# Where the Griffin product and two weight low parts stand in VectorE's program, in a two-layer hybrid decoder trunk

## The chip, the cores and the metric

The kernel runs on one NeuronCore of a Trainium2 chip. The metric is the device time of one execution in microseconds (us). TensorE (PE in the profile) does the matrix products, VectorE (DVE) and ScalarE (ACT) the elementwise work, GpSimd (POOL) a smaller share of it, and SyncE (SP) issues the DMA transfers of the weights.

## The reference, cut to what matters

Two layers, each of them a half-weighted SwiGLU, a token mixer and another half-weighted SwiGLU, on 256 tokens of width 1024. The mixer runs four branches on one normed input: gated DeltaNet, a diagonal state space model (S5), Griffin's gated linear recurrence (RG-LRU) and retention. What the change touches is in two of them:

```python
def hybrid_mixer(hn, ...):
    proj = hn @ w_in          # all inputs of the branches, and the gates' logits
    out_a = gated_deltanet(...); out_b = s5_layer(...)
    out_c = rg_lru_block(...);   out_d = retention(...)
    gates = sigmoid(gate_logits)
    merged = sum(gates * (branches @ w_branch))
    return merged @ w_out

# gated DeltaNet, chunks of 64 tokens
rhs = concatenate([v * beta, k * (beta * exp(gc))])
lower = where(strict, beta * (k @ k.T) * decay, 0)     # decay = exp(gc_i - gc_j)
attn = (q @ k.T) * decay
q_dec = q * exp(gc)
k_dec = k * exp(gc[-1] - gc)
# Griffin
return h * gelu(yb)
```

## The kernel before, in words

Activations lie transposed in on-chip memory, channels on the partitions and the 256 tokens along a row. All weights are streamed from memory once per layer in pieces of 128 x 1024 values (512 KB). A product keeps nearly full float32 accuracy by three passes: weights and inputs are each split into a high and a low part, and `product` (L492 to L494) issues high by high, low input by high weight, high input by low weight.

**The stream of weights.** SP loads piece i into one of 3 slots of `raw`, once the low part of piece i-3 has been taken. ScalarE copies it to the high part `whi` (L908), once TensorE has used piece i-4. VectorE subtracts (`wlo = raw - whi`, L1265); GpSimd does that for a few pieces (L1174). TensorE waits for the low part before it uses a piece. Nothing schedules this by itself: each engine runs a list written out by hand, in which `ahead(unit)` and `split_to(n)` say up to which piece the high or low parts are made at that place. `ahead(unit)` means up to two pieces beyond the last one of that unit.

**The units.** Each `gate(i)` on TensorE is a projection of 256 gate channels: two pieces, g{i}.0 and g{i}.1, 24 products' passes each. Between the gates TensorE does the small products of the branches, the side units. They use three PSUM banks in turn, in a fixed order: ... eb, ktr, vtr, gb0, gb1, kk0, bb0, kk1, bb1, qk0, qk1 ... So gb1 has the bank of ktr, kk0 that of vtr, and bb1 that of kk0: TensorE waits at each until the engine that reads the earlier unit has done so.

**The place of the change.** After the input projections, of which rv is the last, TensorE does eb, gate 0, the transposes of keys and values (ktr and vtr, L663), the decay rows spread over the partitions (gb0 and gb1, in `over_all`, L671), gate 1, kk0, bb0, kk1, bb1 (keys against keys at L684, betas at L671), gate 2, qk0 and qk1 (L684), gate 3, and then six levels of a triangular inverse.

VectorE meanwhile finishes the normed queries and keys (L1536, L1537), forms Griffin's output (L1541, L1542), makes the low parts of g1.0 and g1.1, scales the queries (L1545, `qdec`), reads ktr's bank twice over for the scaled keys (L1558 and L1559, tile `qkvp`), reads vtr's bank for the scaled values (L1564), makes the low parts of g2.0 and g2.1, and reads gb0 and gb1 (L1580). Then it waits for the exponentials of ScalarE (L1107) and multiplies them with kk and bb (L1585 to L1590).

ScalarE evacuates each gate's bank (L1096) and splits Griffin's output for the later merge (L1103). That split is needed only in the merge, which follows gate 15.

Of the kernel before, what the change touches and what calls it, by code (L numbers as in the profile page):

```python
# [31 lines left out]
ALU = mybir.AluOpType  # L32
ACT = mybir.ActivationFunctionType
# [174 lines left out]
def trunk(nc, weights, params, consts, positions, x_in, y_out):  # L208
    ctx = ExitStack()
    with ctx:  # L210
# [6 lines left out]
        def sb(name, cols, dt=F32, over=None, skip=0):  # L217

            if over is None:
                place[name] = place[""]  # L220
                place[""] += -(-cols // 8) * 8
                assert place[""] <= SLAB, place[""]
            else:
                place[name] = place[over] + skip
            return nc.alloc_sbuf_tensor_at(name, [P, cols], dt, offset=base + 4 * place[name])

        def two(name, n=2, t=SEQ, dt=F32, over=None, skip=0):
            return sb(name, n * t, dt, over, skip)[:].rearrange("p (k t) -> p k t", k=n)
# [11 lines left out]
        griffin = wide[:, 30:32, :]  # L240
# [4 lines left out]
        qkv = two("qkv", 6)  # L245
        zz, su, ly = two("zz"), two("su"), two("ly")
# [5 lines left out]
        brh = sb("brh", 8 * SEQ, F32R, over="flat8")[:].rearrange("p (n k t) -> p n k t", n=NB, k=2)  # L252
# [21 lines left out]
        egb, qdec = two("egb"), two("qdec")  # L274
        rows, rowT = two("rows", 1)[:, 0, :], two("rowT", 2, P)
        tmpA, tmpB, tmpC, tmpD, tmpE, tmpF = (two("tmp" + c) for c in "ABCDEF")
# [14 lines left out]
        side = Units(SIDE, psum[4:7])  # L291
# [9 lines left out]
        def S(name):  # L301

            if name in once:
                return once[name]
            if (Now.layer, name) not in per_layer:
                per_layer[Now.layer, name] = nc.alloc_semaphore(f"{name}_{Now.layer}")
            return per_layer[Now.layer, name]

        def since(name, n):

            return once[name], Now.layer * PER_LAYER[name] + n
# [16 lines left out]
        def halves(ap, n=2):  # L328
            return ap.rearrange("p (k t) -> p k t", k=n)
# [39 lines left out]
        def slot(ring, i):  # L369
            s0 = (i % (RAW_SLOTS if ring is raw else SLOTS)) * SLOT  # L370
            return ring[:, s0:s0 + P * numbered(i)[1]]

        def piece_at(name):
            return Now.layer * NP + PIECE_INDEX[name]

        def last_piece(unit):
            return Now.layer * NP + UNIT_PIECES[unit][-1]
# [15 lines left out]
        def r32(ap):  # L393

            return ap.bitcast(F32)
# [495 lines left out]
        def scalar_layer(act):  # L891
            A = nc.scalar.activation
# [18 lines left out]
            def ahead(unit):  # L911

                split_to(last_piece(unit) + 3)
# [175 lines left out]
            def gate(i):  # L1089
                ahead(f"g{i}")  # L1090
                act.wait_ge(S("main"), main.ready(f"g{i}"))
                if i == 11:
                    act.wait_ge(*since("s5x", 8))
                if i == 15:
                    act.wait_ge(S("branch2"), 1)
                A(gates[:, 2 * i:2 * i + 2, :], halves(main.bank(f"g{i}")[:]), ACT.Tanh, scale=0.5).then_inc(S("main_act"), 1)  # L1096
# [2 lines left out]
            act.wait_ge(S("side"), side.ready("eb"))  # L1099
            A(egb, halves(side.bank("eb")[:]), ACT.Exp).then_inc(S("side_act"), 1)  # L1100
            gate(0)
            act.wait_ge(S("griffin"), 1)
            A(brh[:, 2], griffin, ACT.Copy).then_inc(S("branch_high"), 1)  # L1103
            ahead("g1")
            for hp in range(2):
                act.wait_ge(S("side_dve"), side.taken(f"gb{hp}"))
                A(flat(dec)[:, hp, :], flat(dec)[:, hp, :], ACT.Exp).then_inc(S("dec"), 1)  # L1107
            gate(1)
            gate(2)
            gate(3)  # L1110
            for lv in range(LEVELS):
# [138 lines left out]
        def vector_layer(dve):  # L1250
            V = nc.vector
            chain = [0]

            def link(ins):
                chain[0] += 1
                ins.then_inc(S("dve"), 1)
                dve.wait_ge(S("dve"), chain[0])
# [3 lines left out]
            def split_to(n):  # L1261

                for i in [i for i in range(split[0], min(n, DEPTH * NP)) if i % NP in BY_DVE]:
                    dve.wait_ge(once["high"], i + 1)
                    V.tensor_tensor(slot(wlo, i), slot(raw, i), r32(slot(whi, i)), ALU.subtract).then_inc(S("low_dve"), 1)  # L1265
                split[0] = max(split[0], n)

            def ahead(unit):

                split_to(last_piece(unit) + 3)  # L1270
# [265 lines left out]
            V.scalar_tensor_tensor(qkv[:, 0:2, :], qkv[:, 0:2, :], 0.5 * DH ** -0.5, mx_sq[:, 0:2, :], ALU.mult, ALU.mult)  # L1536
            V.scalar_tensor_tensor(qkv[:, 2:4, :], qkv[:, 2:4, :], 0.5, mx_sq[:, 2:4, :], ALU.mult, ALU.mult).then_inc(S("k_normed"), 1)  # L1537
            dve.wait_ge(S("k_normed"), 1)

            dve.wait_ge(S("gelu_t"), 1)  # L1540
            link(V.scalar_tensor_tensor(tmpD, tmpD, 1.0, ly, ALU.add, ALU.mult))  # L1541
            V.scalar_tensor_tensor(griffin, tmpF, 0.5, tmpD, ALU.mult, ALU.mult).then_inc(S("griffin"), 1)  # L1542
            ahead("g0")
            dve.wait_ge(S("side_act"), side.taken("eb"))
            V.tensor_tensor(qdec, qkv[:, 0:2, :], egb, ALU.mult).then_inc(S("dve_q"), 1)  # L1545

            dve.wait_ge(S("side"), side.ready("ktr"))
            dve.wait_ge(S("side_act"), side.taken("rowt"))
# [18 lines left out]
                link(V.tensor_copy(brh[:, n], src))  # L1567
                V.tensor_tensor(brl[n], src, r32(brh[:, n]), ALU.subtract).then_inc(S(f"branch{n}"), 1)

            ahead("g1")  # L1570
            dve.wait_ge(once["masks"], 4)

            for hp in range(2):
                ps = side.bank(f"gb{hp}")
                dve.wait_ge(S("side"), side.ready(f"gb{hp}"))
                for t in range(2):
                    for j in range(2):
                        o = (t * 2 + j) * 64
                        h = 2 * t + hp
                        last = V.tensor_scalar(dec[:, hp, t, j, :], ps[:, o:o + 64], rowT[:, j, h:h + 1], 0.0, ALU.subtract, ALU.min)  # L1580
                last.then_inc(S("side_dve"), 1)
            tj = lambda m, hp: m[:, hp].rearrange("p t j c -> p (t j) c")
            for hp in range(2):
                dve.wait_ge(S("dec"), hp + 1)
# [201 lines left out]
        with nc.Block() as block:  # L1786
# [14 lines left out]
            @block.vector  # L1801
            def _(dve):
                vector_first(dve)
                for Now.layer in range(DEPTH):
                    vector_layer(dve)
                vector_last(dve)

            @block.scalar
            def _(act):
                scalar_first(act)  # L1810
                for Now.layer in range(DEPTH):
                    scalar_layer(act)
# [167 lines left out]
```

## Time and profile before

| | before |
|---|---|
| median of 3 runs | 1367.34 us (1365.52 to 1367.47) |
| the profiled execution | 1367.37 us, span 1365.6 us |
| PE busy | 1318.3 us, 97% |
| DVE busy | 894.7 us, 66% |
| ACT busy | 646.7 us, 47% |
| POOL busy | 246.0 us, 18% |
| mean granted TensorE clock | 0.989 |

The span is the time from the first to the last instruction; 1.8 us of the execution lie outside it. The clock of 1.00 is 2.4 GHz, and 0.50 is 1.2 GHz. In the timeline rows, the first number is the start in us from the span's beginning, the second how long the row's instructions take together, and a bracket names idle time of the engine before it and what ended that.

### The profile page before, as it was taken

The page shows a single profiled execution, that of the slowest core. Times are in us where ns is not written, and L with a number is a line of the kernel's source. Part 1 is how long each engine was busy: PE and PEld are TensorE (multiplying, and loading weights), DVE is VectorE, ACT ScalarE, POOL GpSimd, SP SyncE. Part 2 cuts the span into 40 slices and gives each one's busy share as a digit, 9 for nine tenths or more (in the row PEclk, how much of TensorE's full clock was granted, in tenths as well). Part 3 has the DMA queues.
Part 4 walks back from the last instruction along what each step waited for, and adds up shares of the span by engine and source line. Part 5 has one row for each costly group of instructions (what it writes and reads, how often), then busy time and mean ns, then how long its engine had stood idle before and what let it go on. Part 6 is the DMA issues. An engine that isn't in the chain of part 4 may idle for free. (4 is left out here: it accounts for less than half of the span.)

```text
span 1365.6 us, 27564 instructions
## 1 busy us (share of the span) xinstructions
PE 1318.3 (97%) x11790; PEld 1280.6 (94%) x11790; DVE 894.7 (66%) x1343; ACT 646.7 (47%) x948; POOL 246.0 (18%) x199
## 2 busy tenths in 40 slices
PE   6999999989999999999999999999889999999998
PEld 6999999988788999999999999999877899999997
DVE  7777546876966865555477765568678577655553
ACT  6444647643234454444454455476322354544442
POOL 2000011004833520000210000200166254100000
PEclk9999999999999999999999999999999999999999
DMA  6555654533233545566546556454422335555553
GB/s 233 193 186 187 197 190 143 183 124 106 79 109 109 170 152 188 186 208 207 180 149 188 186 184 194 151 193 145 136 90 67 124 122 168 167 190 188 181 182 117
DMA packets 61321, 220.25 MB, mean 161 GB/s; under 512 B 6928, under 2 KB 7184, under 8 KB 60688
## 3 DMA queue, kind: packets, MB, share of 16 engines
q1 hardware_dynamic: 61200, 218.50, 49.7%
q8 instruction: 93, 1.52, 0.4%
q14 instruction: 28, 0.23, 0.1%
HBM read 217.42 MB, written 1.05 MB: 160 GB/s over the span
## 5 line engine op out<-in xcount | busy, mean ns | idle before, releaser
L492 PE MATMUL bank<-xh,whi 128*128 128x256 f32 x2384 | 676.6, 284 | 5.5 <-DVE wlo L1265 3.8
L493 PE MATMUL bank<-xl,whi 128*128 128x256 f32 x2384 | 669.6, 281 | 0.0
L494 PE MATMUL bank<-xh,wlo 128*128 128x256 f32 x2384 | 668.8, 281 | 0.0
L1265 DVE TENSOR_TENSOR wlo<-raw,whi 128x1024 fp32r<-128x1024 f32 (+1 forms) x382 | 469.2, 1258 | 159.7 <-ACT whi L908 157.6
L908 ACT ACTIVATE whi<-raw 128x1024 fp32r<-128x1024 f32 (+1 forms) x414 | 416.3, 1035 | 108.9 <-DMA raw<-weights 93.6
L492 PEld LDWEIGHTS bank<-xh,whi 128*128 128x128 f32 x2384 | 452.0, 190 | 14.0 <-issue 6.3
L493 PEld LDWEIGHTS bank<-xl,whi 128*128 128x128 f32 x2384 | 451.9, 190 | 0.2
L494 PEld LDWEIGHTS bank<-xh,wlo 128*128 128x128 f32 x2384 | 451.7, 189 | 0.0
L493 PE MATMUL bank<-hl,whi 128*128 128x256 f32 x704 | 196.8, 279 | 0.0
L494 PE MATMUL bank<-hh,wlo 128*128 128x256 f32 x704 | 196.6, 279 | 0.0
L492 PE MATMUL bank<-hh,whi 128*128 128x256 f32 x704 | 196.6, 279 | 0.0
L1215 POOL TENSOR_TENSOR flat<-flat 128x256 f32<-128x256 f32 x36 | 33.6, 932 | 714.7 <-ACT flat L927 713.7
L971 ACT ACTIVATE tmpB<-bank 128x256 f32<-128x256 f32 x88 | 33.8, 385 | 237.7 <-PE bank L494 237.5
L492 PEld LDWEIGHTS bank<-hh,whi 128*128 128x128 f32 x704 | 132.3, 188 | 0.0
L494 PEld LDWEIGHTS bank<-hh,wlo 128*128 128x128 f32 x704 | 132.3, 188 | 0.0
L493 PEld LDWEIGHTS bank<-hl,whi 128*128 128x128 f32 x704 | 132.3, 188 | 0.0
L1304 DVE TENSOR_TENSOR tmpC<-tmpB,bank 128x256 f32<-128x256 f32 x88 | 37.1, 422 | 132.5 <-ACT tmpB L971 132.5
L1174 POOL TENSOR_TENSOR wlo<-raw,whi 128x1024 fp32r<-128x1024 f32 x32 | 78.1, 2447 | 100.8 <-ACT whi L908 100.7
L927 ACT ACTIVATE flat<-x 128x512 f32<-128x512 f32 (+1 forms) x30 | 16.4, 546 | 101.4 <-DVE x L1322 101.4
L1096 ACT ACTIVATE wide<-bank 128x512 f32<-128x512 f32 x32 | 19.1, 597 | 82.6 <-PE bank L494 82.6
L1322 DVE SCALAR_TENSOR_TENSOR x<-bank,x 128x512 f32<-128x512 f32 (+1 forms) x30 | 17.5, 583 | 53.8 <-PE bank L494 53.8
L1193 POOL TENSOR_TENSOR big<-big,cst 128x256 f32<-128x256 f32 x24 | 16.8, 721 | 190.4 <-DVE big L1594 190.4
(351 smaller groups left out, 1261.1 us busy)
## 6 DMA issues: line engine op xcount, KB each, us to landing
raw<-weights SPq DMA_DIRECT2D x350, 512.0 KB, 4.0
raw<-weights SPq DMA_DIRECT2D x64, 448.0 KB, 3.9
cst<-consts SPq DMA_DIRECT2D x1, 1088.0 KB, 11.0
par<-params SPq DMA_DIRECT2D x1, 1072.5 KB, 7.5
par<-params SPq DMA_DIRECT2D x1, 1060.5 KB, 9.0
x<-x_in SPq DMA_DIRECT2D x1, 1024.0 KB, 5.1
y_out<-ret SPq DMA_DIRECT2D x4, 256.0 KB, 2.3
ropec<-positions SPq DMA_DIRECT2D x1, 128.0 KB, 2.1
```

What stands on the lines that cost most here:

```text
L492: mm(out, w[0], a[0], start=start, stop=False)
L493: mm(out, w[0], a[1], start=False, stop=False)
L494: return mm(out, w[1], a[0], start=False, stop=stop)
L908: A(slot(whi, i), slot(raw, i), ACT.Copy).then_inc(once["high"], 1)
L971: A(tmpB[:, m % 2, :], main.bank(f"gu{f}_{m}")[:, 0:SEQ], ACT.Silu).then_inc(S(f"silu{f}"), 1)
L1096: A(gates[:, 2 * i:2 * i + 2, :], halves(main.bank(f"g{i}")[:]), ACT.Tanh, scale=0.5).then_inc(S("main_act"), 1)
L1174: tt(slot(wlo, i), slot(raw, i), r32(slot(whi, i)), ALU.subtract).then_inc(S("low_pool"), 1)
L1193: tt(lowc[:, hp].rearrange("p t j c -> p (t j) c"), low[:, hp].rearrange("p t j c -> p (t j) c"), over(lev[:, lv, 0:64], 4), ALU.mult).the ...
L1215: tt(squared[:, 0, :], squared[:, 0, :], squared[:, k, :], ALU.add).then_inc(S("sq_step" if k < KD - 2 else "sq_added"), 1)
L1265: V.tensor_tensor(slot(wlo, i), slot(raw, i), r32(slot(whi, i)), ALU.subtract).then_inc(S("low_dve"), 1)
L1304: V.tensor_tensor(tmpC[:, m % 2, :], tmpB[:, m % 2, :], ps[:, SEQ:512], ALU.mult).then_inc(S("main_dve"), 1)
L1322: V.scalar_tensor_tensor(x[:, tiles, :], halves(main.bank(unit)[:, 0:n * SEQ], n), scale, x[:, tiles, :], ALU.mult, ALU.add).then_inc(S("m ...
```

## The change

VectorE's program, between the normed keys and the use of the decays: Griffin's product (L1541, L1542) and the scaled queries (L1545) move behind the eight reads of gb0 and gb1. The low parts of g1.0 and g1.1, which stood together ahead of the scaled queries, are taken apart: g1.0's stands ahead of ktr's scaling, g1.1's behind vtr's. Those of g2.0 and g2.1 move behind the scaled queries. ScalarE's split of Griffin's output moves from behind gate 0 to behind gate 1. Every instruction is still there once, with the same operands.

```diff
@@ ScalarE @@
             gate(0)
-            act.wait_ge(S("griffin"), 1)
-            A(brh[:, 2], griffin, ACT.Copy).then_inc(S("branch_high"), 1)
             ahead("g1")
             for hp in range(2):
                 act.wait_ge(S("side_dve"), side.taken(f"gb{hp}"))
                 A(flat(dec)[:, hp, :], flat(dec)[:, hp, :], ACT.Exp).then_inc(S("dec"), 1)
             gate(1)
+            act.wait_ge(S("griffin"), 1)
+            A(brh[:, 2], griffin, ACT.Copy).then_inc(S("branch_high"), 1)
             gate(2)
@@ VectorE @@
             dve.wait_ge(S("k_normed"), 1)
-
-            dve.wait_ge(S("gelu_t"), 1)
-            link(V.scalar_tensor_tensor(tmpD, tmpD, 1.0, ly, ALU.add, ALU.mult))
-            V.scalar_tensor_tensor(griffin, tmpF, 0.5, tmpD, ALU.mult, ALU.mult).then_inc(S("griffin"), 1)
-            ahead("g0")
-            dve.wait_ge(S("side_act"), side.taken("eb"))
-            V.tensor_tensor(qdec, qkv[:, 0:2, :], egb, ALU.mult).then_inc(S("dve_q"), 1)
+            split_to(piece_at("g1.0") + 1)
 
             dve.wait_ge(S("side"), side.ready("ktr"))
...
-            ahead("g1")
+            split_to(piece_at("g1.1") + 1)
             dve.wait_ge(once["masks"], 4)
...
                 last.then_inc(S("side_dve"), 1)
+            dve.wait_ge(S("gelu_t"), 1)
+            link(V.scalar_tensor_tensor(tmpD, tmpD, 1.0, ly, ALU.add, ALU.mult))
+            V.scalar_tensor_tensor(griffin, tmpF, 0.5, tmpD, ALU.mult, ALU.mult).then_inc(S("griffin"), 1)
+            dve.wait_ge(S("side_act"), side.taken("eb"))
+            V.tensor_tensor(qdec, qkv[:, 0:2, :], egb, ALU.mult).then_inc(S("dve_q"), 1)
+            ahead("g1")
             tj = lambda m, hp: m[:, hp].rearrange("p t j c -> p (t j) c")
```

VectorE's program before, from the instruction behind the normed keys to the first use of the decays (`wide` is Griffin's output, `wlo` a low part, `qkvp` the scaled keys and values, `big` the decays):

```order
L1541 SCALAR_TENSOR_TENSOR tmpD<-tmpD,ly 128x512
L1542 SCALAR_TENSOR_TENSOR wide<-tmpF,tmpD 128x512
L1265 TENSOR_TENSOR wlo<-raw,whi 128x1024 x2
L1545 TENSOR_TENSOR qdec<-qkv,egb 128x512
L1558 TENSOR_TENSOR qkvp<-bank,rowT 128x256
L1559 TENSOR_TENSOR qkvp<-bank,rowT 128x256
L1558 TENSOR_TENSOR qkvp<-bank,rowT 128x256
L1559 TENSOR_TENSOR qkvp<-bank,rowT 128x256
L1564 SCALAR_TENSOR_TENSOR qkvp<-bank,rowT 128x256 x2
L1265 TENSOR_TENSOR wlo<-raw,whi 128x1024 x2
L1580 TENSOR_SCALAR big<-bank,rowT 128x64 x8
L1585 TENSOR_TENSOR big<-big,cst 128x256
```

The same stretch of VectorE's program in the changed kernel (its line numbers are lower by 6 where the Griffin lines used to stand ahead):

```order
L1265 TENSOR_TENSOR wlo<-raw,whi 128x1024
L1552 TENSOR_TENSOR qkvp<-bank,rowT 128x256
L1553 TENSOR_TENSOR qkvp<-bank,rowT 128x256
L1552 TENSOR_TENSOR qkvp<-bank,rowT 128x256
L1553 TENSOR_TENSOR qkvp<-bank,rowT 128x256
L1558 SCALAR_TENSOR_TENSOR qkvp<-bank,rowT 128x256 x2
L1265 TENSOR_TENSOR wlo<-raw,whi 128x1024
L1574 TENSOR_SCALAR big<-bank,rowT 128x64 x8
L1577 SCALAR_TENSOR_TENSOR tmpD<-tmpD,ly 128x512
L1578 SCALAR_TENSOR_TENSOR wide<-tmpF,tmpD 128x512
L1580 TENSOR_TENSOR qdec<-qkv,egb 128x512
L1265 TENSOR_TENSOR wlo<-raw,whi 128x1024 x2
```

Ahead of the four reads of ktr's bank there stood two Griffin instructions, two low parts and the scaled queries; now one low part stands there. The rest follows behind, the same instructions up to L1585 in all.

ScalarE's program before, from the evacuation of gate 0 to that of gate 1 (`brh` is the high part of Griffin's output, `whi` that of a weight piece, `big` the exponentials of the decays):

```order
L1096 ACTIVATE wide<-bank 128x512
L1103 ACTIVATE brh<-wide 128x512
L908 ACTIVATE whi<-raw 128x1024 x2
L1107 ACTIVATE big<-big 128x256 x2
L1096 ACTIVATE wide<-bank 128x512
```

And in the changed kernel:

```order
L1096 ACTIVATE wide<-bank 128x512
L908 ACTIVATE whi<-raw 128x1024 x2
L1105 ACTIVATE big<-big 128x256 x2
L1096 ACTIVATE wide<-bank 128x512
L1108 ACTIVATE brh<-wide 128x512
```

One instruction moved, past two high parts, two exponentials and one evacuation. TensorE's program is the same in both kernels.

## Rows read from the trace of the kernel before

**Rows 1.** The page, busy time of each engine (share of span, instructions):

```profile
PE 1318.3 (97%) x11790; PEld 1280.6 (94%) x11790; DVE 894.7 (66%) x1343; ACT 646.7 (47%) x948; POOL 246.0 (18%) x199
```

**Rows 2.** Who PE waited for, whole span: total us, times, longest:

```profile
PE bank L671 <- DVE qkvp L1559: 7.8, 2, 4.0
PE bank L731 <- DVE tmpD L1610: 7.2, 4, 2.3
PE bank L492 <- DVE wlo L1265: 3.8, 7, 1.0
```

**Rows 3.** Timeline of PE in layer 0, side products only:

```profile
285.57 1.03 PE L663 MATMUL bank<-cst,qkv 128*128 128x128 f32 x8
286.54 0.65 PE L671 MATMUL bank<-rows,cst 32*64 32x128 f32 x8
291.04 1.12 PE L671 MATMUL bank<-rows,cst 32*64 32x128 f32 x8 [3.85 <-DVE qkvp L1559]
299.95 0.68 PE L684 MATMUL bank<-qkv 64*64 64x64 f32 x16
301.75 0.65 PE L671 MATMUL bank<-rows,cst 32*64 32x128 f32 x8
```

**Rows 4.** Timeline of DVE in layer 0:

```profile
285.37 0.69 DVE L1541 SCALAR_TENSOR_TENSOR tmpD<-tmpD,ly 128x512 f32<-128x512 f32 x1
286.70 2.35 DVE L1265 TENSOR_TENSOR wlo<-raw,whi 128x1024 fp32r<-128x1024 f32 x2
288.97 0.68 DVE L1545 TENSOR_TENSOR qdec<-qkv,egb 128x512 f32<-128x512 f32 x1
289.58 0.42 DVE L1558 TENSOR_TENSOR qkvp<-bank,rowT 128x256 f32<-128x256 f32 x1
290.57 0.41 DVE L1559 TENSOR_TENSOR qkvp<-bank,rowT 128x256 f32<-128x256 f32 x1
295.37 0.41 DVE L1585 TENSOR_TENSOR big<-big,cst 128x256 f32<-128x256 f32 x1
300.75 0.42 DVE L1587 TENSOR_TENSOR big<-bank,big 128x256 f32<-128x256 f32 x1 [4.96 <-PE bank L684]
301.67 0.42 DVE L1585 TENSOR_TENSOR big<-big,cst 128x256 f32<-128x256 f32 x1
302.12 0.42 DVE L1587 TENSOR_TENSOR big<-bank,big 128x256 f32<-128x256 f32 x1
```

**Rows 5.** Windows, layer 0: us, busy of PE, PEld, DVE, ACT, POOL, clock, DMA, GB/s:

```profile
287.19:291.04 3.85, 0.00 (x0) 0.00 (x1) 3.85 (x8) 1.21 (x2) 0.00 (x0) 0.84 0.57 148
291.04:299.95 8.91, 8.91 (x57) 8.45 (x57) 4.75 (x13) 1.89 (x3) 0.00 (x0) 0.68 0.52 173
301.75:308.14 6.39, 6.39 (x60) 6.08 (x57) 3.45 (x6) 0.79 (x1) 0.00 (x0) 1.00 0.44 138
```

**Rows 6.** Windows, layer 1, the same three stretches:

```profile
959.94:963.92 3.98, 0.00 (x1) 0.01 (x1) 3.98 (x8) 1.33 (x2) 0.00 (x0) 0.79 0.55 150
963.92:972.62 8.70, 8.70 (x56) 8.24 (x56) 4.74 (x13) 1.89 (x3) 0.00 (x0) 0.70 0.49 174
974.43:980.82 6.39, 6.39 (x62) 6.09 (x58) 3.45 (x5) 0.79 (x1) 0.00 (x0) 1.00 0.46 148
```

**Rows 7.** Timeline of DVE in layer 1:

```profile
958.24 0.69 DVE L1541 SCALAR_TENSOR_TENSOR tmpD<-tmpD,ly 128x512 f32<-128x512 f32 x1
968.25 0.41 DVE L1585 TENSOR_TENSOR big<-big,cst 128x256 f32<-128x256 f32 x1
```

**Rows 8.** Timeline of ACT in layer 0:

```profile
291.60 1.06 ACT L908 ACTIVATE whi<-raw 128x1024 fp32r<-128x1024 f32 x1 [3.20 <-DMA raw<-weights]
295.49 0.42 ACT L1107 ACTIVATE big<-big 128x256 f32<-128x256 f32 x1 [0.35 <-DVE big L1580]
```

**Rows 9.** Windows, layer 0: a half gate with its small products, twice:

```profile
323.23:326.84 3.61, 3.61 (x42) 3.41 (x40) 3.38 (x6) 1.33 (x2) 0.00 (x0) 1.00 0.34 129
330.29:335.41 5.12, 5.12 (x41) 4.87 (x41) 4.35 (x4) 1.33 (x2) 4.98 (x3) 0.67 0.30 102
```

## The prediction, made before the changed kernel ran

> **What bounds the kernel now.** I read the page's busy times first. TensorE is busy for 97% of the span, VectorE for 66% [rows 1], so a change of VectorE's order can be worth only what TensorE loses by waiting. The second view is the list of TensorE's waits. The largest entry on this part of the program is L671 waiting for VectorE's L1559, 7.8 us in 2 waits [rows 2]: once a layer, TensorE stands before gb1, whose bank is that of ktr, until the last of the four instructions that scale the transposed keys has read it. The third view is the timeline around it. In layer 0 TensorE ends gb0 at 286.54 + 0.65 = 287.19 and starts gb1 at 291.04 [rows 3]; VectorE's last read of ktr's bank ends at 290.57 + 0.41 = 290.98, so TensorE follows 0.06 us behind it [rows 4].
>
> The fourth view, windows over the stall and what follows, shows a second cost. The granted clock averages 0.84 within the stall, so it fell from 1.00 to 0.50 (2.4 to 1.2 GHz) before the stall was over, and 0.68 over the gate behind it. gb1 and gate 1 together take 8.91 us; bb1 and gate 2, the same 8 small and 48 large products at full clock, take 6.39 us [rows 5]. In layer 1 the stall is 3.98 us and the gate takes 8.70 against 6.39 us [rows 6]. So the waits cost 7.8 us and the half clock behind them 2.52 + 2.31 = 4.83 us.
>
> **The change part by part.**
>
> *Ahead of ktr's scaling.* VectorE's path from the normed keys to ktr's first read holds before: two Griffin instructions, two low parts, the scaled queries. L1541 starts at 285.37 and L1558 at 289.58, 4.21 us later. After: one low part. Two of them take (288.97 - 286.70) / 2 = 1.14 us each to the next instruction's start [rows 4]. ktr's first read then starts at 285.37 + 1.14 = 286.51. The transposes start at 285.57 and all eight take 1.03 us, so ktr's four are there at about 286.1, ahead of it by 0.4 us [rows 3]. The last read ends as far behind the first as before, 290.98 - 289.58 = 1.40 us: at 287.91, and gb1 starts at 287.97, 3.07 us earlier. The stall is left with 287.97 - 287.19 = 0.78 us. In layer 1 L1541 starts at 958.24 [rows 7], so gb1 starts at 958.24 + 1.14 + 1.40 + 0.06 = 960.84, against 963.92 [rows 6]: 3.08 us earlier, and 0.90 us of the stall are left.
>
> *The clock behind it.* With 0.78 and 0.90 us of stall left I take the clock to stay at full. In layer 0 it fell late in a stall of 3.85 us: if it went to 0.50 at once, an average of 0.84 means that 0.32 of the stall was at half, so it fell 2.6 us into it; in layer 1, by 0.79, 2.3 us [rows 5, 6]. Neither point is reached by a stall below 1 us. gb1 and gate 1 then take 6.39 us, and kk0 starts at 287.97 + 6.39 = 294.36 against 299.95: 5.59 us earlier. In layer 1 at 960.84 + 6.39 = 967.23 against 972.62: 5.39 us. The other bound is that the clock falls as it did: then only 3.07 and 3.08 us are gained.
>
> *The low part of g1.1.* It now follows vtr's scaling: two instructions of about 0.33 us from start to start, as the four before them (L1558 at 289.58, the fourth at 290.57). It ends near 287.83 + 0.66 + 1.2 = 289.7. TensorE wants it for the second half of gate 1, near 287.97 + 0.58 + 2.9 = 291.4. It is hidden with 1.7 us of cover.
>
> *Griffin, scaled queries, low parts of g2.0 and g2.1 behind the reads of gb0 and gb1.* VectorE runs without a gap from 285.37 to the start of L1585 at 295.37 [rows 4], and the same instructions stand in between after the change, so L1585 starts at 295.37 still, unless one waits. None should: the high part of g2.1 waits on ScalarE for its transfer, which begins when the low part of g1.0 is done. Before, that low part ended near 287.9 and the copy started at 291.60 [rows 8], 3.7 us on; now it ends near 286.6, and the copy starts near 290.3. The exponentials follow it on ScalarE and end near 290.3 + 1.06 + 0.42 + 0.3 = 292.1, instead of 295.9 [rows 8]. The low part of g2.0 is done near 294.3 and that of g2.1 near 295.4; gate 2 wants the first at 296.9.
>
> *What is late next.* Before, L1585 stood at VectorE's head long before kk0 came; it then idled 4.96 us [rows 4]. Now kk0 comes at 294.36 and VectorE is the later one. TensorE goes kk0, bb0, kk1, bb1, with bb1 1.80 us behind kk0 (301.75 - 299.95) [rows 3], so at 296.16, and bb1 has kk0's bank. VectorE reads kk0 in L1587, which starts 0.45 us behind L1585 (302.12 - 301.67) and takes 0.42 us [rows 4]: it ends at 296.24, and TensorE can start bb1 at 296.30. A new wait of 0.14 us, and the same in layer 1 (968.25 + 0.45 + 0.42 + 0.06 = 969.18 against 967.23 + 1.80 = 969.03, 0.15 us). Queued behind bb1 is gate 2 alone. The bounds of this term are 0 and, were one low part more in front of L1585, 1.3 us.
>
> *ScalarE's split of Griffin's output.* One instruction goes behind gate 1's evacuation and ahead of the high parts of g3.0 and g3.1. It waits for nothing, as Griffin's product ends near 292.6 and gate 1 near 294.4. g3.0's high part comes near 295.4 to 296.5, and gate 3 wants it near 304. I cost it at nothing; ScalarE is idle for most of a gate. SP's queue and the transfers stay in their order, and g3.1's low part would come near 300, wanted near 307.
>
> *The sum.* 5.59 - 0.14 = 5.45 us in layer 0, 5.39 - 0.15 = 5.24 us in layer 1: 10.7 us. From gate 2 on every wait of the mixer hangs on a product of TensorE, so the whole program moves forward by that. The profiled execution took 1367.37 us (span 1365.6), which is the median of the runs, 1367.34, within 0.03 us: 1367.34 - 10.7 = 1356.6 us.
>
> **The rivals.**
>
> *A: the clock still falls once behind the rest of the stall.* For it: before gate 1 TensorE does only small products, and a wait of 2.29 us at L731 was enough for a half gate to take 5.12 instead of 3.61 us [rows 9]. Against it: a rest of 0.8 to 0.9 us. One such dip costs 1.5 us: 1358.1 with one layer, 1359.6 with both. The Trainium skill, "TensorE: Matmul & The Clock Gate", Part 1, holds that the monitor behind the clock runs freely beside the program, so that where the clock turns can differ from run to run. By that rule A could strike in some runs only; the trace, with the same stall cooling the clock in both layers, neither bears it out nor excludes it.
>
> *B: the dips further on come elsewhere.* The program behind the stall is shifted by 5 us in layer 0 and by 11 in layer 1, and the 2.29 us wait at L731 could then fall so that the clock holds. For it: the waits of L731 total 7.2 us in 4, and two cost a dip [rows 2, 9]. Against it: in the trace both layers show the same. Each dip that goes saves 1.5 us, two give 1353.6; a new one costs as much.
>
> *C: the ring of weights becomes the bound.* The stall and the slow gate gave the transfers over 5 us a layer in which to catch up. For it: L492 waits for low parts 7 times, up to 1.0 us [rows 2]. Against it: 3.7 us from a free slot to the copy, with three slots, is under half of what three pieces take TensorE (9 us). If three gates a layer each had a wait of 1.0 us 6 us of the gain would be lost: 1362.6.
>
> *D, slower: bb1 takes the stall over.* The chain is low part of g1.0, transfer and high part of g2.1, the exponentials, L1585, L1587, bb1. It has 295.37 - 292.1 = 3.3 us to spare. Beyond that each us is a wait before gate 2, and a long one brings the half clock's 2.5 us with it. The gain is then gone when the chain is 3.3 + 5.3 - 2.5 = 6.1 us late, which takes a transfer of 10 us instead of 3.7. At 8 us late it is 1.9 us a layer slower, 1371 us. Against it: 3.20 us is the whole wait for that transfer now [rows 8].
>
> *E: L1559 isn't what holds gb1* (the releaser is inferred), and the stall stays: 1367. Against it: TensorE follows its end by 0.06 us in layer 0, and the bank is ktr's.
>
> **How the numbers follow.** The forecast of 10.7 us has 0.71, A 0.12, B (a dip fewer) 0.07, C 0.05, D 0.03, E 0.02. Its own range is 1355 to 1358.5. The range of 1353.2 to 1361.0 takes in A and B with both layers and the bounds of the new wait; left out are C, D, E and some of the scatter of 2 us between runs. About 0.2%, 2.7 us, is what a measurement of this kernel can tell from no change. Faster by more than that are the forecast, A, B and C: 0.95; E is within: 0.02; D slower: 0.03.
>
> **What the profile after would show.** Right: the wait at L671 of 0.7 to 1.0 us in each layer, the clock at 1.00 in gate 1, kk0 5.4 to 5.6 us earlier in layer 0 and 10.6 to 10.9 in layer 1, a wait before bb1 of under 0.3 us, none at L492 for g1.1. Wrong: a stall of over 2 us before gb1, a clock of 0.5 in gate 1, or a new row of L492 behind L1265 in gates 1 to 3.

## The result, and the profile after

| | before | changed | ratio |
|---|---|---|---|
| median, first comparison (5 runs each) | 1367.34 us | 1355.48 us | 0.9929 (0.9909 to 0.9949) |
| median, second comparison (8 and 5 runs) | 1366.65 us | 1354.84 us | 0.9908 (0.9892 to 0.9925) |
| span of the profiled execution | 1365.6 us | 1353.7 us | |

The changed kernel is faster by 11.9 us between the medians of the first comparison and by 11.8 between those of the second; 10.7 were forecast, and both times lie inside the range of 1353.2 to 1361.0 us. Put into us, the two ratios are gains of 9.7 (7.0 to 12.4) and 12.6 (10.2 to 14.8) us. The ten runs of the changed kernel go from 1352.29 to 1360.28 us.

The list of TensorE's waits in the changed kernel, total us, times and longest, answers to [rows 2]:

```profile
PE bank L731 <- DVE tmpD L1610: 7.2, 4, 2.3
PE bank L492 <- DVE wlo L1265: 3.8, 7, 1.0
PE bank L671 <- DVE qkvp L1553: 1.7, 2, 0.9
```

The wait for the scaled keys went from 7.8 to 1.7 us, and the two others didn't move. No other entry of the list grew by more than the 0.6 us of TensorE's first wait, at the start of the program (10.9 to 11.5): nothing took the stall's place. TensorE's timeline in layer 0, side products only, against [rows 3]:

```profile
286.27 1.03 PE L663 MATMUL bank<-cst,qkv 128*128 128x128 f32 x8
287.23 0.65 PE L671 MATMUL bank<-rows,cst 32*64 32x128 f32 x8
288.72 0.65 PE L671 MATMUL bank<-rows,cst 32*64 32x128 f32 x8 [0.84 <-DVE qkvp L1553]
295.15 0.68 PE L684 MATMUL bank<-qkv 64*64 64x64 f32 x16
```

From gb0 to gb1 it is 1.49 us where it was 4.50, and from gb1 to kk0 6.43 where it was 8.91. The windows over the stall and over gb1 with gate 1 (us, busy of PE, PEld, DVE, ACT, POOL, clock, DMA, GB/s) show why, against [rows 5]:

```profile
287.88:288.72 0.84, 0.00 (x1) 0.00 (x0) 0.84 (x4) 0.13 (x1) 0.00 (x0) 1.00 0.66 78
288.72:295.15 6.43, 6.43 (x56) 6.12 (x56) 6.40 (x16) 1.71 (x3) 0.00 (x0) 1.00 0.50 155
```

The granted clock is 1.00 in both, where it was 0.84 and 0.68. VectorE in the same stretch, against [rows 4]:

```profile
286.12 1.23 DVE L1265 TENSOR_TENSOR wlo<-raw,whi 128x1024 fp32r<-128x1024 f32 x1
287.26 0.42 DVE L1552 TENSOR_TENSOR qkvp<-bank,rowT 128x256 f32<-128x256 f32 x1
288.26 0.41 DVE L1553 TENSOR_TENSOR qkvp<-bank,rowT 128x256 f32<-128x256 f32 x1
296.12 0.42 DVE L1585 TENSOR_TENSOR big<-big,cst 128x256 f32<-128x256 f32 x1
296.57 0.42 DVE L1587 TENSOR_TENSOR big<-bank,big 128x256 f32<-128x256 f32 x1
```

It is again without a gap: 10.00 us from the low part at 286.12 to L1585 at 296.12, as from 285.37 to 295.37 before. L1587 ends at 296.99. In layer 1, TensorE's rows show what is left of the stall and the wait at bb1:

```profile
952.93 0.65 PE L671 MATMUL bank<-rows,cst 32*64 32x128 f32 x8
954.49 0.65 PE L671 MATMUL bank<-rows,cst 32*64 32x128 f32 x8 [0.91 <-DVE qkvp L1553]
960.87 0.68 PE L684 MATMUL bank<-qkv 64*64 64x64 f32 x16
961.49 0.65 PE L671 MATMUL bank<-rows,cst 32*64 32x128 f32 x8
962.07 0.68 PE L684 MATMUL bank<-qkv 64*64 64x64 f32 x16
962.82 0.65 PE L671 MATMUL bank<-rows,cst 32*64 32x128 f32 x8
```

gb1 to kk0 is 6.38 us where it was 8.70, and bb1 starts 1.95 us behind kk0 instead of 1.81 (in layer 0, 1.90 instead of 1.80).

TensorE's program is the same in both kernels, so each of its 11,790 products can be set against its own start before. In layer 0 the changed kernel is at +0.69 us at gb0, -2.32 at gb1, -4.80 at kk0 and -4.70 at bb1, behind its new wait: 5.39 us gained. In layer 1 it is at -6.36 us at gb0, -11.75 at kk0 and -11.61 at bb1: 5.25 us gained. The two make 10.64 us. Between the two layers the difference goes from -4.70 to -6.36 us, most of it evenly over the first SwiGLU of layer 1, and behind layer 1's mixer it gains another 0.25 us; neither program changed there.

### The profile page after: what moved, and what is told of

It is laid out like the page before. It is cut to its first block and busy times, and to the rows that moved or that the text cites. A ratio compares the mean times of both kernels' runs of the same rounds, so it can differ in the third digit from the quotient of the medians.

```text
span 1353.7 us, 27564 instructions
## 1 busy us (share of the span) xinstructions
PE 1312.7 (97%) x11790; PEld 1275.1 (94%) x11790; DVE 894.7 (66%) x1343; ACT 647.4 (48%) x948; POOL 245.7 (18%) x199
## 5 line engine op out<-in xcount | busy, mean ns | idle before, releaser
L1114 ACT ACTIVATE big<-bank 128x256 f32<-128x256 f32 x24 | 9.2, 385 | 84.2 <-PE bank L731 84.1
```

## The experiments

Each experiment ran in one of three comparisons with the kernel before, whose median was 1367.26 us beside the first four (parts alone, 30 products, both low parts), 1364.95 us beside the next four (15 products, Griffin and low parts, GpSimd, half gate) and 1366.65 us beside the last three. The ratios are to the kernel before of the same comparison. A "fall" of the clock below is its going from 1.00 to 0.50 for a stretch. Line numbers in the text are those of the changed kernel.

### VectorE's part alone

```diff
 (changed kernel, ScalarE)
             gate(0)
+            act.wait_ge(S("griffin"), 1)
+            A(brh[:, 2], griffin, ACT.Copy).then_inc(S("branch_high"), 1)
             ahead("g1")
...
             gate(1)
-            act.wait_ge(S("griffin"), 1)
-            A(brh[:, 2], griffin, ACT.Copy).then_inc(S("branch_high"), 1)
```

> VectorE's order as in the changed kernel, ScalarE's Griffin split left behind gate 0. My theory: gb1 still starts early and gate 1 runs at full clock, so the main gain stands; but ScalarE now waits for Griffin's product ahead of the high parts of g2.0 and g2.1 and of the exponentials, VectorE's L1585 comes about 1.3 us later and bb1 waits 1.4 instead of 0.1 us. So 1.3 us a layer of the gain are lost: about 1358 to 1359 us, 8 to 9 us faster than before. Rival (ScalarE's split was the reason for the gain): no gain, 1367 us, stall before gb1 of 3.9 us.

Measured: 1359.16 us, ratio to before 0.9945 (0.9929 to 0.9961). ScalarE's timeline in layer 0 has the wait:

```profile
292.79 0.63 ACT L1103 ACTIVATE brh<-wide 128x512 fp32r<-128x512 f32 x1 [6.20 <-DVE wide L1578]
293.33 1.99 ACT L908 ACTIVATE whi<-raw 128x1024 fp32r<-128x1024 f32 x2
295.22 0.71 ACT L1107 ACTIVATE big<-big 128x256 f32<-128x256 f32 x2
```

And TensorE's timeline, layer 1, what came of it:

```profile
956.63 0.65 PE L671 MATMUL bank<-rows,cst 32*64 32x128 f32 x8 [0.91 <-DVE qkvp L1553]
963.01 0.68 PE L684 MATMUL bank<-qkv 64*64 64x64 f32 x16
966.09 0.65 PE L671 MATMUL bank<-rows,cst 32*64 32x128 f32 x8 [1.20 <-DVE big L1587]
974.02 0.97 PE L684 MATMUL bank<-qkv 64*64 64x64 f32 x32
```

gb1 to kk0 is 6.38 us as in the changed kernel, so VectorE's order alone makes the main gain. The wait at bb1 came, 1.20 us where I had expected 1.4; what I had not expected is that it brought the half clock: bb1 and gate 2 take 7.93 us instead of 6.4. Product by product, the two together put TensorE back by 2.6 us in each layer.

### ScalarE's part alone

```diff
 (kernel before, ScalarE)
             gate(0)
-            act.wait_ge(S("griffin"), 1)
-            A(brh[:, 2], griffin, ACT.Copy).then_inc(S("branch_high"), 1)
             ahead("g1")
...
             gate(1)
+            act.wait_ge(S("griffin"), 1)
+            A(brh[:, 2], griffin, ACT.Copy).then_inc(S("branch_high"), 1)
```

> VectorE's order as before, ScalarE's Griffin split behind gate 1. My theory: the stall before gb1 stays 3.9 us with the half clock behind it, no change of the time within 0.5 us. Rival (ScalarE's split was the reason for the gain): faster by 5 us or more.

Measured: 1366.18 us, ratio 1.0000 (0.9987 to 1.0012). The stall stays, 3.79 and 3.92 us, and gb1 to kk0 takes 8.54 and 9.47 us. The edit is worth nothing that could be measured alone; beside VectorE's it is worth what the first experiment lacks, about 3.7 us between the medians. That is less than twice 2.6 us; in the first experiment's trace two falls of the clock that the changed kernel has further on, 1.6 us each, are missing.

### The stall filled with products

```diff
 (kernel before, TensorE)
             over_all("gb0", 0, 0)
+            ps = main_bank("g1")
+            for _ in range(30):
+                mm(ps[:, 0:P], ident, ident, start=True, stop=True)
             over_all("gb1", 0, 1)
```

> Before, with 30 small products of constants put on TensorE between gb0 and gb1, into the bank that gate 1 overwrites; they take about 3.3 us and end before the stall does. My theory (the stall costs twice, as waiting and as half clock behind it): gb1 starts at the same place, gate 1 runs at full clock and takes 6.4 with gb1, so 2.3 to 2.5 us a layer are gained, 1362.5 us. Rival (the slow gate had another cause than the stall, or such small products don't hold the clock): 1367 us and gate 1 at 0.5 to 0.7 of the clock.

Measured: 1367.31 us, ratio 1.0003 (0.9984 to 1.0022). It missed, for a reason in the edit: TensorE's timeline shows 60 instructions for 30 products, which take 6.96 us instead of the 3.3 that I had counted on.

```profile
288.50 0.65 PE L671 MATMUL bank<-rows,cst 32*64 32x128 f32 x8
289.08 6.96 PE L690 MATMUL bank<-cst 128*128 128x128 f32 x60
295.98 0.65 PE L671 MATMUL bank<-rows,cst 32*64 32x128 f32 x8
302.36 0.68 PE L684 MATMUL bank<-qkv 64*64 64x64 f32 x16
```

gb1 comes 7.48 us behind gb0 instead of 4.50, but reaches kk0 in 6.38. The same with `range(15)`:

> Before, with 15 instead of 30 constant products between gb0 and gb1. The 30 took 6.96 us, twice what I had counted on, and put gb1 off by 3.1 us, about what the clock gave back; 15 take 3.5 us and end inside the stall of 3.85 us. My theory: gb1 starts as before, gb1 and gate 1 take 6.4 us at full clock instead of 8.9 and 8.7, 4.8 us faster in all: 1362.5 us. Rival (the half clock behind the stall costs nothing in the end): 1367 us.

Measured: 1361.52 us, ratio 0.9970 (0.9953 to 0.9988).

```profile
286.78 0.65 PE L671 MATMUL bank<-rows,cst 32*64 32x128 f32 x8
287.36 3.62 PE L690 MATMUL bank<-cst 128*128 128x128 f32 x30
291.35 0.65 PE L671 MATMUL bank<-rows,cst 32*64 32x128 f32 x8 [0.38 <-DVE qkvp L1562]
297.74 0.68 PE L684 MATMUL bank<-qkv 64*64 64x64 f32 x16
```

gb1 stands 4.57 us behind gb0, where it was 4.50 before, and kk0 6.39 us behind gb1 instead of 8.91 (6.38 instead of 8.70 in layer 1). So the slow gate was the stall's doing, and is worth 4.8 us in the trace with gb1 no earlier than before. The median is 3.4 us below that of before, and the ratio's interval, 1.6 to 6.4 us, holds the 4.8.

### More work ahead of ktr's scaling

Two steps back from the changed kernel: both low parts ahead, and both low parts and Griffin's product ahead.

```diff
 (changed kernel, VectorE; both low parts ahead)
-            split_to(piece_at("g1.0") + 1)
+            ahead("g0")
...
-            split_to(piece_at("g1.1") + 1)
 (the second: Griffin's two instructions also back ahead of ahead("g0"))
```

> The changed kernel, with the low part of g1.1 put back ahead of ktr's scaling beside that of g1.0. My theory: gb1 starts 1.14 us later, the stall is 2.0 us, the wait at bb1 goes, and 1.0 us a layer are lost: 1357.5 us if the clock holds, 1360.5 us if a stall of 2.0 us makes it fall once in each layer. Rival (only ahead-of-time low parts matter, not the stall's length): same time as the changed kernel.

Measured: 1361.41 us, ratio 0.9959 (0.9943 to 0.9975).

> The changed kernel, with Griffin's product and both low parts of gate 1 put back ahead of ktr's scaling; the scaled queries stay behind. My theory: stall of 0.85 + 1.14 + 1.34 = 3.3 us, gb1 2.5 us later than in the changed kernel, and a fall of the clock behind it: 1363.5 us if the fall is as long as that behind the stall of 2.0 us, 1365 us if it is as long as before. Rival (the fall's cost grows with the stall's length alone): between the two, without steps.

Measured: 1365.74 us, ratio 1.0002 (0.9987 to 1.0016). TensorE's timelines in layer 0, first of the one and then of the other:

```profile
286.88 0.65 PE L671 MATMUL bank<-rows,cst 32*64 32x128 f32 x8
289.09 0.65 PE L671 MATMUL bank<-rows,cst 32*64 32x128 f32 x8 [1.56 <-DVE qkvp L1553]
297.02 0.68 PE L684 MATMUL bank<-qkv 64*64 64x64 f32 x16
```

```profile
291.03 1.11 PE L671 MATMUL bank<-rows,cst 32*64 32x128 f32 x8 [3.12 <-DVE qkvp L1556]
300.09 0.68 PE L684 MATMUL bank<-qkv 64*64 64x64 f32 x16
```

| us in layers 0 and 1 | idle before gb1 | granted clock in it | start of gb1 to start of kk0 |
|---|---|---|---|
| before | 3.85, 3.98 | 0.84, 0.79 | 8.91, 8.70 |
| before, ScalarE's part alone | 3.79, 3.92 | 0.74, 1.00 | 8.54, 9.47 |
| both low parts and Griffin ahead | 3.12, 3.37 | 0.86, 1.00 | 9.06, 7.96 |
| both low parts ahead | 1.56, 1.99 | 1.00, 1.00 | 7.93, 7.92 |
| changed | 0.84, 0.91 | 1.00, 1.00 | 6.43, 6.38 |
| changed, second profile | 0.71, 0.86 | 1.00, 1.00 | 6.43, 6.39 |
| changed, with the half gate of below | 0.72, 0.91 | 1.00, 1.00 | 6.38, 7.95 |

The wait grows with what stands ahead. The clock's price, what gb1 to kk0 takes above 6.39 us, is nothing, 1.5 to 1.6 us, or 2.2 to 3.1 us. In the dearest cases (both layers of the first two rows, layer 0 of the third) the price and what the half clock took within the wait (one minus the granted clock, times the wait) add up to the same: 2.52 + 0.16 x 3.85, 2.15 + 0.26 x 3.79 and 3.08 + 0 are 3.1 us, and so are the other two within 0.1. So the dearer price is least where the clock falls early in the wait. A stall of 3.12 us paid it in layer 0 and one of 3.37 only the lower one in layer 1, so it isn't set by the length alone. Against before, the second of the two kernels should gain 1.9 us by its trace, which its times, with a ratio of 1.0002, don't show.

### No low part ahead of ktr's scaling

```diff
 (changed kernel, VectorE)
-            split_to(piece_at("g1.0") + 1)
```

> The changed kernel with both low parts of gate 1 behind the scaling of keys and values. My theory: ktr's scaling starts when its transposes are there, the stall before gb1 goes from 0.84 to about 0.5 us, but the low part of g1.0 comes 0.9 us later than gate 1 wants it, a new wait at L492; 0.6 us a layer slower than the changed kernel, no fall of the clock. Rival (the low part of g1.0 is in the way and has cover, as that of g1.1 has): 0.3 us a layer faster.

Measured: 1359.22 us, ratio 0.9944 (0.9931 to 0.9957). TensorE in layer 0:

```profile
289.91 0.65 PE L671 MATMUL bank<-rows,cst 32*64 32x128 f32 x8 [0.55 <-DVE qkvp L1552]
291.79 0.36 PE L492 MATMUL bank<-xh,whi 128*128 128x256 f32 x1 [1.24 <-DVE wlo L1265]
299.12 0.68 PE L684 MATMUL bank<-qkv 64*64 64x64 f32 x16
```

The stall shrank to 0.55 us and the new wait came, 1.24 us where I had expected 0.9; but it brought the half clock, and gb1 to kk0 takes 9.21 us with the wait in it. So it is 4.4 us slower than the changed kernel beside it (1354.84) and not 1.2. The one low part ahead of ktr earns its place.

### The low part of g1.0 on GpSimd

```diff
 (changed kernel)
-           if _n.startswith("mg") or _n in [...] + ["gu1_0.0", "wo0.0", "wo1.0"]]
+           if _n.startswith("mg") or _n in [...] + ["g1.0", "gu1_0.0", "wo0.0", "wo1.0"]]
```

> The changed kernel, with the low part of g1.0 made by GpSimd, which is idle there. My theory: ktr's scaling starts when its transposes are there, 0.9 us earlier than now at most 0.3 to 0.7 us of which reach gb1 (stall of 0.2 to 0.6 us instead of 0.84), the wait at bb1 goes; 0.4 to 0.8 us a layer faster: 1354.4 us, within the scatter of the runs, so the trace decides. Rival: GpSimd's low part slows VectorE or comes late, and TensorE waits for it at gate 1.

> The changed kernel with the low part of g1.0 on GpSimd, again, beside the changed kernel on the same chip. The trace of the first showed gb1 0.3 us earlier and nothing late. My theory: 0.3 us a layer, 0.7 us in all, which the times can't tell from none. Rival: slower by 1 us or more.

Measured: 1355.41 and 1355.60 us, ratios 0.9918 (0.9891 to 0.9946) and 0.9916 (0.9902 to 0.9930). The trace of the first has gb1 with 0.54 us of idle time before it instead of 0.84, held now by the transposes (VectorE's first read at 288.21, with the transposes from 287.52); the second has 0.55 in both layers. The wait at bb1, which I had expected to go, stays at 0.1 us: kk0 comes earlier by as much as VectorE does. The times can't tell it from the changed kernel, 1355.48 and 1354.84.

### A half gate ahead of a longer wait

```diff
 (changed kernel, TensorE, in the levels)
                 for hp in range(2):
+                    late = (lv, hp) in ((1, 1), (2, 1))
+                    if late:
+                        half(f"g{4 + lv}", hp)
...
-                    half(f"g{4 + lv}", hp)
+                    if not late:
+                        half(f"g{4 + lv}", hp)
```

> The changed kernel; in levels 1 and 2 of the triangular inverse TensorE does the second half gate ahead of the small product that waits for VectorE (2.29 and 1.30 us at L731) instead of behind it. My theory, that of a stall costing twice: the stall of 2.29 us goes and with it the half clock's 1.5 us, that of 1.30 us goes too, and TensorE waits about 0.7 us for ScalarE's copy ahead of the next small product in both: 3.0 + 0.6 = 3.6 us a layer, 1348.3 us. Rival (the chain of VectorE and GpSimd through the S5 states sets the pace of the levels): the wait comes back at L711 or in the next level, 1354 us or more.

Measured: 1358.62 us, ratio 0.9938 (0.9915 to 0.9960), where the kernel with a low part on GpSimd had 1355.41 us in the same comparison. The rival was right. TensorE's waits:

```profile
PE bank L711 <- POOL tmpF L1212: 6.4, 4, 2.0
PE bank L734 <- DVE tmpD L1614: 6.0, 4, 1.7
PE bank L746 <- ACT big L1118: 1.9, 4, 0.5
```

L734 is L731 of the changed kernel, where TensorE waited 7.2 us in all; L711 waited 2.7 us there. The three entries went from 9.9 to 14.3 us together. By the releasers that the trace names, GpSimd's work on the S5 states sets the pace there, and TensorE only met it elsewhere; that this chain is the limit is argued from them and not tested.

This trace shows something more. Up to the levels the program is that of the changed kernel, and in layer 1 the rest of the stall is the same 0.91 us, yet the clock fell 1.75 us behind its end. The windows over the wait and over gb1 with gate 1:

```profile
954.66:955.56 0.90, 0.00 (x0) 0.00 (x0) 0.90 (x4) 0.11 (x1) 0.00 (x0) 1.00 0.30 82
955.56:963.46 7.90, 7.90 (x56) 7.64 (x56) 7.78 (x17) 1.75 (x3) 0.00 (x0) 0.78 0.42 137
```

kk0 starts at 963.51, 7.95 us behind gb1 instead of 6.38. That is rival A of the prediction, in one layer of one execution.

### The changed kernel again

> The changed kernel once more. In the profiles so far each long stretch of TensorE's large products has one of two steps, 116.67 or 117.78 ns a product, from stretch to stretch and run to run, whatever the kernel; the first profile of the changed kernel had the quicker step where that of before had the slower. My theory: the program's own gain is 10.7 us and the rest of the 11.9 us was this and the start; over more runs the median stands 10 to 11.5 us below that of before. Rival (the changed kernel has the quicker step by nature): 12 us or more below, and the quicker step in all stretches again.

Measured: 1354.84 us, 11.8 us below before, ratio 0.9908 (0.9892 to 0.9925). That is above my 10 to 11.5 us and below the rival's 12, so the time decides nothing; the profile speaks for my theory. The windows over the first SwiGLU of layer 0, in the first profile of the changed kernel and in this one, differ in the count of products:

```profile
30.00:190.00 160.00, 160.00 (x1374) 160.00 (x1373) 109.06 (x186) 79.18 (x112) 3.08 (x3) 1.00 0.61 193
```

```profile
30.00:190.00 160.00, 160.00 (x1360) 160.00 (x1360) 108.48 (x184) 78.66 (x112) 3.09 (x3) 1.00 0.59 191
```

The profiled execution is the slowest of the five, with a span of 1358.3 us against 1353.7 of the first profile. Most of the 4.6 us come at one place, the merge of layer 1:

```profile
1103.59 2.64 DVE L1561 CAST brh<-tmpB 128x512 fp32r<-128x512 f32 x1
1106.26 2.87 DVE L1562 TENSOR_TENSOR brl<-tmpB,brh 128x512 fp32r<-128x512 f32 x1
```

In the first profile these two take 0.43 and 0.69 us. Here each begins just behind the start of a low part on GpSimd (1103.54 and 1106.23); TensorE waits 2.49 us for the second, the clock falls, and the place costs 3.6 us. It lies outside the change.

## Why the prediction was right

**The stall, right.** It had gb1 3.07 us earlier against the transposes and 0.78 us of stall left. From the transposes' start to gb1's it was 5.47 us (291.04 - 285.57) and is 2.45 (288.72 - 286.27): 3.02 us. What is left is 0.84 and 0.91 us.

**The clock behind it, right in size, its reason wrong, and partly luck.** 2.48 and 2.32 us came back in gb1 and gate 1, against 2.52 and 2.31 of the forecast, and the filled stall gives them back alone. But I took the clock to be safe since it had fallen 2.3 to 2.6 us into the stalls before. The other traces show that it can fall when the wait is over: 0.67 us behind the end of a stall of 1.56 us, 0.39 and 0.92 us behind waits of 1.20 us ahead of bb1, and 0.97 us behind a wait of 1.24 us. It even fell once behind the rest of the stall that the change leaves, 0.91 us, in the kernel with the half gate. TensorE has this rest (0.71 to 0.91 us) in eight places of four traces, those of the changed kernel twice, of VectorE's part alone and of the half gate, and the clock fell behind one of them. So rival A is real and strikes in some executions; that neither profile of the changed kernel has it is in part luck, and how many of its ten runs paid the 1.5 us isn't known. With one low part more ahead of ktr both layers paid: TensorE lost 2.2 and 2.6 us, where the wait alone grew by 0.7 and 1.1.

**Low parts and what is late next, right.** TensorE's waits for low parts are 3.8 us in 7 as before, VectorE's row of 10.00 us stayed, and the wait before bb1 is 0.10 and 0.14 us, against 0.14 and 0.15. C, D and E didn't come.

**ScalarE's split, right.** Costed at nothing where it stands now, which holds. Left where it was, it costs 2.6 us a layer in the trace, as the exponentials stand behind it; the prediction gave no price for that.

**Dips further on (B), not in the changed kernel's first profile, but real.** The clock's four falls, behind the waits of 2.29 us at L731 and of 1.3 us at L786, stand in the profiles before and after. In the other traces they come and go, with no edit near them: of 26 waits of 1.28 to 1.30 us at L786, in the two layers of the 13 traces, 18 had a fall behind them, and of 26 waits of 0.96 us at L525 6 had one. So a dip more or less belongs to the scatter between runs, for the kernel before too.

**The sum.** 5.45 and 5.24 us were forecast for the two layers, and 5.39 and 5.25 are in the trace. The other 1.2 us of the 11.9 between the two profiled executions are a start later by 0.7 us and a drift of 1.9 us the other way where neither program changed. The gains by the ratios, 9.7 and 12.6 us, have 10.7 us between them, so the times hold nothing that the forecast lacks. They don't confirm it to better than 2 us either: that it agrees with the trace to 0.1 us is the stronger evidence.

## What to carry to other kernels

Where engines take banks in turn, look for what a full engine has queued ahead of the read that frees a bank, and put ahead of it only what TensorE wants sooner. Price a TensorE stall twice, as the wait and as the slow products behind it: here 1.2 us of wait cost 1.5 us more, and 3.8 to 4.0 us cost 2.2 to 3.1. Don't take a short rest of a stall for safe because one profile shows the full clock behind it: 0.91 us kept it in two traces and lost it in a third. When one engine's product moves back, move its reader on the next engine back too, if others queue behind that reader; and ask of each stall that you take away whether another chain sets the pace there, as at L711. Set two traces of the same program against each other product by product: it tells the change's own gain from what scatter adds elsewhere.

## What the runs showed of the hardware that was not expected

**The same wait doesn't always cost the clock.** At the 2.29 us waits at L731 the clock fell in all 24 places (12 traces without the half gate's edit), from 0.5 us ahead of the wait's end to 1.6 us behind it; behind the 1.3 us waits at L786 in 18 of 26, behind waits of 0.96 us at L525 in 6 of 26, and behind the second waits at L731, 1.3 us as well, in none of 26. So the length of a wait doesn't decide it alone, and with the same program around it the clock fell in one execution and not in the next. What decides it no run here separates.

**Large products have two steps.** At a granted clock of 1.00 the mean from one start to the next has two values, each constant over a stretch of 150 us: 116.67 or 117.78 ns. In 160 us of the first SwiGLU of layer 1 that is the 1361 products before against 1374 in the changed kernel:

```profile
710.00:870.00 160.00, 160.00 (x1361) 160.00 (x1360) 104.96 (x164) 76.78 (x108) 6.08 (x6) 1.00 0.59 187
```

```profile
710.00:870.00 160.00, 160.00 (x1374) 160.00 (x1373) 104.89 (x155) 77.68 (x105) 6.16 (x6) 1.00 0.59 189
```

Which value a stretch has changes from run to run, for the changed kernel as for others, and is worth 1.5 us in such a stretch. What sets it no run here shows.
